# First half of a pooling stage and norm moved beside the last gathers, and four FFN blocks in plain fp32

## What is computed

```python
def block_fn(args):                                   # PEER
    tb, ib, gb = args
    u = u_tab[ib]
    act = jax.nn.gelu(jnp.einsum("td,thkd->thk", tb, u), approximate=False)
    vv = v_tab[ib]
    return jnp.einsum("thk,thkd->td", gb * act, vv)
x = _rmsnorm(x, normf_g)
for i in range(2):
    h = _modulate(_rmsnorm_2(x, norm_w[i, 0]), sh1, sc1)
    y = _pool_mixer(h, pool_w, pool_b, pool_scale)    # i == 0: window mean minus token, 256x256 per group
    x = x + g1 * y
    u = _modulate(_rmsnorm_2(x, norm_w[i, 1]), sh2, sc2) @ w_up
    up = u[t-1] * conv_w[0] + u[t] * conv_w[1] + u[t+1] * conv_w[2] + conv_b
    a, v = jnp.split(up, 2, axis=-1)
    x = x + g2 * ((silu(a) * v) @ w_down)
```

## Time and profile before

| what | us |
|---|---|
| median of 3 runs | 1671.11 |
| lowest, highest | 1670.04, 1671.52 |
| the profiled execution | 1669.39 |
| its span, first to last instruction | 1667.6 |

### The profile page before, as it was taken

How to read it: one execution, slowest core, us unless ns; L and a number is a source line. 1 busy time by engine, 2 the same in 40 slices (tenths; PEclk the granted TensorE clock), 3 DMA queues, 4 the chain that set the end, 5 groups by cost and what they waited for, 6 DMA issues and landing times.

```text
span 1667.6 us, 22193 instructions
## 1 busy us (share of the span) xinstructions
PE 1478.8 (89%) x8310; PEld 1059.6 (64%) x8310; DVE 1106.1 (66%) x2162; ACT 583.5 (35%) x847; POOL 824.9 (49%) x746
## 2 busy tenths in 40 slices
PE   8999999766565699999888885889999999999999
PEld 7997675654221266665443441438999896799987
DVE  4865633798488877877756675417886557468864
ACT  6653331211121222221100001127665454466652
POOL 0025230376767765656667777742675113036640
PEclk9999999987977899999799997999999999999999
DMA  7447860598999999999999999994555545635551
GB/s 281 152 151 301 318 253 26 210 389 304 393 407 371 409 401 402 402 403 403 401 401 394 409 396 402 406 396 161 171 187 190 189 182 222 243 111 202 176 191 38
DMA packets 154252, 477.15 MB, mean 286 GB/s; under 512 B 10017, under 2 KB 12321, under 8 KB 150945
## 3 DMA queue, kind: packets, MB, share of 16 engines
q0 software_dynamic: 73728, 268.47, 41.2%
q1 hardware_dynamic: 80416, 207.27, 34.0%
HBM read 474.65 MB, written 1.05 MB: 285 GB/s over the span
## 4 chain that ended last, share of the span: by engine, by line
PE 54%; DMA 13%; DVE 11%; POOL 10%; issue 5%; ACT 2%; DVEq 0%; ACTq 0%; POOLq 0%
PE ps L673 53%; DMA arena<-in_peer_v,cl 11%; POOL arena L2802 8%; DVE arena L1851 2%; PE ps L677 1%; POOL wring L2802 1%; DVE arena L1466 1%; DMA wring<-in_peer_v,cl 1%; DVE arena L1472 1%; DVE wring L1851 1%; DMA wring<-in_peer_u,arena 1%; DVE arena L1469 0%; DVE cvb L1472 0%; DVE arena L1781 0%; ACT arena L2190 0%
## 5 line engine op out<-in xcount | busy, mean ns | idle before, releaser
L673 PE MATMUL ps<-arena,wring 128*128 128x256 f32 (+2 forms) x2360 | 596.0, 488 | 106.0 <-DMA arena<-in_peer_v,cl 101.2
L673 PEld LDWEIGHTS ps<-arena,wring 128*128 128x128 f32 (+1 forms) x2360 | 333.0, 168 | 352.7 <-DMA arena<-in_peer_v,cl 179.7
L1851 DVE CUSTOM_DVE_ANT_0 arena<-arena 128x1024 f32<-128x1024 f32 x214 | 257.6, 1226 | 134.8 <-DMA arena<-in_peer_u,arena 131.9
L2802 POOL DMA_INDIRECT arena<-in_peer_u,arena x214 | 240.0, 1121 | 192.4 <-DVE arena L1809 78.2
L2802 POOL DMA_INDIRECT arena<-in_peer_v,cl x214 | 229.2, 1071 | 77.3 <-issue 60.4
L673 PE MATMUL ps<-hhl,wh 128*128 128x256 f32 (+1 forms) x1056 | 252.4, 323 | 1.2 <-POOL hhl L2812 0.7
L2190 ACT ACT_TABLE_LOAD x64 | 82.1, 1283 | 392.9 <-DVE arena L1851 266.1
L1466 DVE TENSOR_TENSOR wl<-wring,wh 128x2048 fp32r<-128x2048 f32 (+1 forms) x76 | 168.1, 2212 | 60.0 <-ACT wh L2193 58.2
L673 PE MATMUL ps<-hhl,wl 128*128 128x256 f32 x704 | 198.7, 282 | 0.0
L673 PEld LDWEIGHTS ps<-hhl,wh 128*128 128x128 f32 x1056 | 175.8, 190 | 19.5 <-POOL hhl L2812 2.5
L2193 ACT ACTIVATE wh<-wring 128x2048 fp32r<-128x2048 f32 (+1 forms) x78 | 146.1, 1874 | 70.7 <-PE ps L673 68.9
(11 more groups left out here) (257 smaller groups left out, 2025.4 us busy)
## 6 DMA issues: line engine op xcount, KB each, us to landing
wring<-in_ups SPq DMA_DIRECT2D x33, 2048.0 KB, 9.2
wring<-in_ada SPq DMA_DIRECT2D x24, 2048.0 KB, 9.9
wring<-in_ffn_w_down SPq DMA_DIRECT2D x12, 2048.0 KB, 9.0
wring<-in_w_in SPq DMA_DIRECT2D x8, 2048.0 KB, 8.3
wring<-in_ffn_w_down SPq DMA_DIRECT2D x6, 1536.0 KB, 7.6
wring<-in_peer_wq SPq DMA_DIRECT2D x4, 2048.0 KB, 16.1
wring<-in_attn_w_qkv SPq DMA_DIRECT2D x4, 2048.0 KB, 8.4
wring<-in_w_out SPq DMA_DIRECT2D x2, 2048.0 KB, 9.7
```

Of the source, the lines that this page charges most:

```text
L673: return pe.matmul(o, l, r, start=start, stop=stop)
L1851: ve.tensor_tensor_reduce(out=o, in0=o, in1=h2[:, t, :], scale=1.0, scalar=0.0, op0=MUL, op1=ADD, accum_out=dots[j % 2][:, k:k + 1]).then_ ...
L2802: po.indirect_dma_start(out=ring[n % NR], out_offset=None, in_=table, in_offset=bass.IndirectOffsetOnAxis(ap=which, axis=0)).then_inc(S[f" ...
```

## The change

Tokens 0 to 119 get their pooling stage and second norm ahead of the end of the gathers. A third list, `first`, is given to `woven` on PE, DVE and ACT, with 14 places between rest 458 and rest 517: the sums over the bands and the final norm's factors, then transposes, window products, pool products (120 columns), the norm's column sums, and on DVE and ACT the scaling and shift of these columns. Its rows lie in other memory (`y_a`, `z_a`). The pool weights are loaded into slot 1 ahead of the wait for `p_v` 248.

Behind the gathers PE begins with the first 120 columns of FFN blocks 0 and 1 in plain fp32 (`first_tokens`); then come window, transpose and pool products for tokens 120 to 255 (136 columns), the first 120 columns of block 2 on both sides of the norm sums (where four filler products stood), those of block 3, and then the other 136 columns of the four blocks (`direct_part`). Blocks 4 to 21 stay split; their pieces are counted from 0 again, so all later counts fall by four. The four direct blocks need no piece and no adding of a low sum; the pieces of blocks 4, 5 and 6 are prepared behind the norm and in `after` of blocks 0 to 2. The diff, cut:

```diff
-    nfb, junk = hpC[:, 1568:2592], hpC[:, 2592:3616]
+    nfb, y_a = hpC[:, 1568:2592], hpC[:, 2592:3616]
+    z_a = junk = hpC[:, 3616:4640]
+    NA, NB = 120, 136
...
-            if n == 496:
-                yield ("window_sums",)
-            elif n in (500, 504, 508):
-                yield "rows", (n - 500) // 4
+            if n == 500:
+                yield ("cleared",)
...
+    def woven(peer, context, first):
...
+        places = [458, 462, 466, 490, 492, 495, 497, 500, 502, 505, 508, 511, 514, 517]
...
+                if places and n == places[0]:
+                    places.pop(0)
+                    next(first, None)
...
-        nth[0] = 0
+        nth[0] = 1
+        load("pool", ("p_pl", 4), pool_w(), n=3)
         sp.wait_ge(*at("p_v", 248))
-        load("pool", ("p_pl", 4), pool_w(), n=3)
...
-                load(("up", l, g), split_done(n0 + 2 * g + 1), up(l, g), n=3)
+                direct = l == 0 and 2 * g < DIRECT
+                load(("up", l, g), ("p_dir", 2 * g + 2) if direct else split_done(n0 + 2 * g + 1), up(l, g), n=3)
...
-            busy(spread[:, 256:384], 4)
+            if between:
+                between()
+            else:
+                busy(spread[:, 256:384], 4)
...
+        def first_half():
+
+            pe.wait_ge(*at("d_l", 48))
+            for n in range(2):
+                b = take(("zb", n), "a_sz", 1)
+                for e in range(2):
+                    mm(b[:, 256 * e:256 * e + 256], ones, bands[2 * n + e][0], e == 0, False)
+                    k = mm(b[:, 256 * e + 120:256 * e + 256], ones, bands[2 * n + e][1], False, e == 1)
+            k.then_inc(S["p_zb"], 1)
+            for _ in range(3):
+                yield
+            pe.wait_ge(*at(*rows_at(0, "scaled")))
+            for q in range(2):
+                b = take(("xT", 0, q), "a_mb", q + 1)
+                for j in range(4):
+                    k = tr(b[:, c128(j)], y_a[:, c128(4 * q + j)])
+                k.then_inc(S["p_xT"], 1)
+
+            def windows_a(js):
+                for j in js:
+                    b = take(("wda", j), "v_pl", j + 1)
+                    for e in range(2):
+                        k = mm(b[:, 256 * e:256 * e + NB], z_a[:, c128(2 * j + e)], bands[j][0][:, 0:NB], True, True)
+                    k.then_inc(S["p_wda"], 1)
+
+            windows_a((0, 1))
+            yield
+            windows_a((2, 3))
+            yield
+            for half in range(2):
+                pooled(half, range(2 * half, 2 * half + 2))
+                yield
+            for _ in range(2):
+                yield
+            b = take("crsa", "a_crsa", 1)
+            pe.wait_ge(*at("a_csq", 4))
+            for c in range(8):
+                k = mm(b[:, 0:NA], ones, sqb[:, c, 0:NA], c == 0, c == 7)
+            k.then_inc(S["p_crsa"], 1)
+            yield
+
+        def pooled(t, gs, name="pla", n0=0, cols=slice(0, 120)):
+
+            w = weights("pool")[:, 0:2048].rearrange("p (g c) -> p g c", g=8)
+            n = cols.stop - cols.start
+            for g in gs:
+                pe.wait_ge(*at("v_pl", n0 + g + 1))
+                b = take((name, g), "v_px", 2 * n0 + 2 * g + 2)
+                for j in range(2):
+                    for kk in range(2):
+                        k = mm(b[:, 256 * j:256 * j + n], w[:, 2 * g + kk, c128(j)], sqb[:, 2 * g + kk, cols], kk == 0, kk == 1)
+                k.then_inc(S["p_" + name], 1)
+
         ring8[0] = [0, 1, 2, 3, 4, 7]
-        woven(peer(), context())
+        woven(peer(), context(), first_half())
...
+        direct = {}
+
+        def direct_part(f, i, cols):
+
+            w = weights(("up", 0, f // 2)).rearrange("p (k i c) -> p k i c", k=8, i=2)
+            for kk in range(8):
+                if f == i == 0 and cols.start:
+                    pe.wait_ge(*at("a_mid", mids(1, kk)))
+                k = mm(direct[f][:, 256 * i + cols.start:256 * i + cols.stop], w[:, kk, i, c128(f % 2)], sqb[:, kk, cols],
+                       kk == 0, kk == 7)
+            return k
+
+        def first_tokens(f, i):
+
+            if i == 0:
+                direct[f] = take(("up", 0, f), "v_up", f + 1, keep=True)
+                where["up", 0, f] = direct[f][:, 0:256], direct[f][:, 256:512]
+            direct_part(f, i, slice(0, NA))
+
+        pe.wait_ge(*at("a_cid", 32))
+        for f in range(2):
+            for i in range(2):
+                first_tokens(f, i)
+        wd = [take(("wd", j), "v_pl", 4 + j + 1) for j in range(4)]
         pe.wait_ge(*at("v_add", 2))
+        pe.wait_ge(*at(*rows_at(1, "pool")))
+        for j in range(4):
+            for e in range(2):
+                k = mm(wd[j][:, 256 * e:256 * e + NB], zrows[:, 1, c128(2 * j + e)], bands[j][1], e == 0, e == 1)
+            k.then_inc(S["p_wd"], 1)
+        pe.wait_ge(*at(*rows_at(1, "scaled")))
         for q in range(2):
             held[5 + q] = "a_mb", 3 + q
-        turned_rows(1, ps[5:7])
-        ring8[0] = list(range(7))
-        w = weights("pool")[:, 0:2048].rearrange("p (g c) -> p g c", g=8)
-        for g in range(4):
-            pe.wait_ge(*at("v_pl", g + 1))
-            b = take(("pl", g), "v_px", 2 * g + 2)
-            for j in range(2):
-                for kk in range(2):
-                    k = mm(b[:, 256 * j:256 * j + 256], w[:, 2 * g + kk, c128(j)], sqb[:, 2 * g + kk, :], kk == 0, kk == 1)
-            k.then_inc(S["p_pl"], 1)
+            where["xT", 1, q] = ps[5 + q]
+            for j in range(4):
+                k = tr(ps[5 + q][:, c128(j)], yrows[:, 1, c128(4 * q + j)])
+            k.then_inc(S["p_xT"], 1)
+        ring8[0] = list(range(8))
+        pooled(1, range(4), "pl", 4, slice(NA, 256))
...
+            start = 0
+            if l == 0:
+                start = DIRECT
+                first_tokens(2, 0)
+                token_norms(m, lambda: first_tokens(2, 1))
+                for i in range(2):
+                    first_tokens(3, i)
+                for f in range(DIRECT):
+                    for i in range(2):
+                        k = direct_part(f, i, slice(NA, 256))
+                    k.then_inc(S["p_dir"], 1)
+                    del kept["up", 0, f]
+                ring8[0] = list(range(7))
+            else:
+                token_norms(m)
+            for n in range(start, 22):
...
+                if l > 0 or blk >= DIRECT:
+                    ve.wait_ge(*at("a_lw", low_sums(l, blk)))
+                    k = tt(b[0][:, 0:256], b[0][:, 0:256], cv[:, 0, :], ADD)
+                    told(k, "v_us", low_sums(l, blk))
+                if l == 0 and blk in (1, 2):
+                    prepare(blk + 4)
+                elif blk > (4 if l == 0 else 0):
                     prepare(blk + 2)
...
+                scaled(m, lambda c: sqb[:, c, NA:256])
+                low = row_lo(rows_of[m], ffx[l], sqb)
+                for c in range(0, 8, 2):
+                    low(c)
+                prepare(DIRECT)
+            else:
+                scaled(m, lambda c: sqb[:, c, :], row_lo(rows_of[m], ffx[l], sqb, lambda c: mod(l, 3, c, 0)))
+                prepare(2)
...
+                direct = l == 0 and blk < DIRECT
+                ac.wait_ge(*at(*(("p_dir", blk + 1) if direct else ("p_u", n0 + blk + 1))))
                 if blk > 1:
                     ac.wait_ge(*at("g_act", 22 * l + blk - 1))
-                k = copy(cv[:, 0, :], where["up", l, blk][0][:, 256:512])
-                told(k, "a_lw", 22 * l + blk + 1)
+                if not direct:
+                    k = copy(cv[:, 0, :], where["up", l, blk][0][:, 256:512])
+                    told(k, "a_lw", low_sums(l, blk))
                 if blk > 0:
                     gate(blk - 1)
-                ac.wait_ge(*at("v_us", 22 * l + blk + 1))
+                if not direct:
+                    ac.wait_ge(*at("v_us", low_sums(l, blk)))
                 told(conv_mid(l, where["up", l, blk], cv, blk), "a_cv", 22 * l + blk + 1)
-                prepare(blk + 3)
+                if l == 0 and blk < 2:
+                    prepare(blk + 5)
+                elif not direct:
+                    prepare(blk + 3)
```

More of the change, by code:

```diff
@@ L101, in program @@
     ctx = ExitStack()
+    DIRECT = 4
     GOES_ON = {
@@ L1964, in context, with windowed, added_pool, first_half @@
             yield from modulated_c(2, lambda c: hcT[:, c, :], 1, 0)
-        woven(peer(), context())
+        def windowed(t, gs):
+            for g in gs:
+                ve.wait_ge(*at(("p_wda", "p_wd")[t], g + 1))
+                for e in range(2):
+                    c = 2 * g + e
+                    part = sqb[:, c, NA * t:NA * t + NB]
+                    k = stt(part, where[("wda", "wd")[t], g][:, 256 * e:256 * e + NB], AD[:, 0, 0, 0, c:c + 1], part, MUL, ADD)
+                told(k, "v_pl", 4 * t + g + 1)
+        def added_pool(t, gs):
+            o = slice(NA * t, (NA, 256)[t])
+            for g in gs:
+                ve.wait_ge(*at(("p_pla", "p_pl")[t], g + 1))
```

(72 more changed lines are left out.)

215 lines of the change are left out of this document (83 added, 132 removed).

## The result

The changed kernel takes 1679.29 us (median of 5 runs, 1677.09 to 1681.05) against 1671.05 beside it: a ratio of 1.0048, with a 95% interval of 1.0033 to 1.0063, that is 8.0 us slower (5.5 to 10.5). The forecast was 8.0 us slower, 1679.

The account below looks back on a forecast made before the run. Bound: in the last 60 us PE's order decides when gathers may be issued; later, PE itself. 2.8 + 5.6 - 0.4 = 8.0 us slower: 1677.4 against 1669.39, 1679 on the median's scale; range 1672.5 to 1684.

Parts of the forecast that it names:

- Part 1: Among the late gathers: the 1 MB pool weights, loaded earlier into a full DMA queue, cost 2.8 us (1.5 to 2.9).
- Part 2: Ahead of row 480: PE's inserted transposes, window and pool products delay gather issues, cost 5.6 us (3.0 to 6.6).
- the 0.7 us taken off for backlog at the end: At the last gathers: DMA backlog left there reduces the 6.3 us delay of gather 492's issue by 0.7.
- T: The moment PE's last products behind the gathers end, 1119.46 us before; forecast 8.4 us later, at about 1128.
- Part 3: From T to the steady FFN blocks: gain of about 0.4 us (ends: gain 3, loss 3.5).
- The wait ahead of block 7: In the FFN blocks: block 7 misses its low part by about 1.8 us, ACT waiting for POOL's late products.
- The first: Rival: the ring of twelve buffers hides the stops, POOL waits under 1 us at gather 492; 4.3 us faster; chance 0.08.
- The second: Rival: only the first POOL stop reaches the data (2.9), load paid, refund 2.5; 3.2 us slower; chance 0.14.
- a refund of 2.5: Time won back behind T, as the second rival put it; the first rival put it at 7.1 us.
- The third: Rival: up weights come at T + 4.7 and PE, having waited, runs slower; about 12.5 us slower; chance 0.15.
- Its price of 1.5 us for the lower clock: In the third rival: PE at its lower clock level after waiting loses some 1.5 us, read behind a 4.50 us wait.

Follow-up runs that it names:

- E1: The kernel before with only the pool weights' load moved ahead, right behind the context's last load; 1672.84 us, 1.0022.
- E6: Changed kernel with block 6's split behind block 2's convolution, windows at rest 482, transposes and pool products from rest 505; 1670.02 us, 1.0003.
- E13: E6 without the pool weights' load, its pool products reading what an earlier load left in the slot; 1665.9 us, 0.9983.
- E2: The kernel before with only PE's transposes, window and pool products inserted at the change's places, on constants, read by nobody; 1676.81 us, 1.0042.
- E8: The changed kernel run again unchanged, as reference on another chip; 1679.24 us, 1.0061 to the kernel before.
- E12: The kernel before with eight more products of 136 columns at rest 482, in PE's wait for gather 464; 1671.02 us, 1.0013.
- E10: E6 with the second load of up weights waiting until all 256 v rows are used instead of 248; 0.9999.
- E7: E6 with the pool weights issued later, when 218 v rows are used; 1670.68 us, 1.0006.

## Why the prediction was right

**Part 1, the megabyte: 2.8 forecast, 3.7 measured (E1, 2.0 to 5.2), 3.2 to 4.3 by the traces.** The mechanism is the one given: bytes among gathers that fill the DMA. The size was short, and so was the bound of 2.9: PE starts on gather 464 3.2 us later in E1 than before, and 3.1 later in E6 than in E13, which differ by the load alone. The 0.6 us of clock behind it and the last 0.5 us are not shown to be the megabyte's (E1). One reading was off: the load does not stand in front of gathers 464 to 467. In the changed kernel it is issued at 997.81 and lands 35.4 us later, before 464 is issued at 1047.62; it holds 464 back through the gathers ahead of that.

**Part 2, PE's inserted work: 5.6 forecast, 5.7 at the last sums (E2), 7.0 by the times (4.7 to 9.2).** The mechanism is the one given. That the two sizes agree to 0.1 is partly luck, since about 0.5 us of the 5.7 was lost ahead of the products. The issue of 486 was to come 3.0 us later and comes 3.3 later, 492 6.3 and comes 7.0. The shape of the stops was off: I put one of 6 us ahead of 486 and missed that the work at place 490 also stands ahead of rows 472 and 473, which gather 484 waits for. So it is 2.9 and 4.3 us, then 4.0 instead of 3. Their sum at the issue was nearly right, and the 0.7 us taken off for backlog at the end were 1.3 (7.0 at the issue, 5.7 at the last sums).

**T.** Forecast 8.4 later, at about 1128; it is 1129.30, 9.8 later on the trace's own scale and 10.6 counted from gather 400. By E1 and E2 the miss is mostly part 1's.

**Part 3, behind the last sums: gain of 0.4 forecast; a loss of 0.4 in the profiled execution, a gain of 1.1 in E8's.** Step by step: the up weights are there 1.15 us behind T (2.4); pool products end at 1146.0, T + 16.7 (16.6); block 4 starts at T + 44.1 (44.0). Block 5 waits 2.63 us (1.9), by the way that was named: the load for block 6, issued when block 1 has been used (T + 35.8; forecast 35.6), takes 10.29 us, then 1.93 on ACT, 2.30 on DVE and the taps. I had taken 8.9 from the earlier trace rows, the median of eight loads of the kernel before and not this load. By the rule of the Trainium skill that I set against it (DMA: Bandwidth & Descriptors, section on the anatomy of one DMA; an estimate of 6.8 us) block 5 would not have waited: the measurement decides, and it is further off than the row. The wait ahead of block 7 did not come (1.8 forecast): PE has none behind block 5. In its place the clock fell behind block 5's wait in the profiled execution, which cost 1.5 us against E8. Two errors of nearly one size cancelled there.

**The rivals.** The first needed a stop under 1 us ahead of 492; it is 3.98. The second needed PE's products to cost 2.9 us and a refund of 2.5; they cost 5 to 6 (E2), and the refund lay between -0.4 and 1.1. The third needed PE to wait 4.7 us for the up weights; it waited 1.15, and the clock stayed at 1.00 behind it. Its price of 1.5 us for the lower clock did not hold even where it was read, ahead of the key product (E12). E6 shows what was right in the first: with the steps in other places the stop ahead of 492 is gone, and what is left is the megabyte against the 4 us behind T, as that rival had said, only that the megabyte is nearly as large as the gain.

That the total is 8.0 forecast and 8.0 measured is luck. E1 and E2 add up to 10.7 us by the times and 10.0 at the last sums, the two profiled executions differ by 10.3 (1679.66 against 1669.39), and the same program run again (E8) is 10.1 us slower (7.8 to 12.4). All of this lies in the range, and the direction and the two causes are shown; the size is known to about 2 us.

## What to carry to other kernels

Work that is moved ahead to use an engine's idle time must be put where that engine waits, counted on its own list: PE waited about 4 us ahead of gather 464 and hardly at all in the forty us behind it; the products cost 5 to 6 us there (E2) and 0.7 in the pause and behind the late stretch (E13's last sums, one trace). Where a ring of buffers ties an engine's order to the issue of transfers, look for every transfer whose buffer stands behind the inserted step, not only for the first that stopped before. And bytes have a price of their own: a load that is moved from a slack stretch into one where the DMA is full is paid whole, whatever hides the rest.

## What the runs showed of the hardware

The clock behind a wait of PE is not a fixed price. Ahead of block 5 PE waited 2.63 us in the changed kernel's trace and 2.55 in E8's, the same program in another run; over the next 3.6 us the granted clock was 0.55 in the one and 1.00 in the other. The two rows (columns as above; PEclk is the third from the end):

```profile
1181.90:1185.50 3.60, 3.57 (x12) 3.04 (x13) 1.69 (x4) 1.93 (x4) 1.86 (x3) 0.55 1.02 393
```

E8:

```profile
1181.80:1185.40 3.60, 3.56 (x22) 3.21 (x23) 1.68 (x4) 1.93 (x4) 1.87 (x3) 1.00 1.04 397
```

The same with the windows in the pause ahead of gather 464, where PE had done the same work in each: behind 2.4 us of waiting the clock stayed at 1.00 in E6 and E10; it fell in E7 behind 2.23 us, and in E13, with E6's order on PE, behind 2.46 (0.51 over the next 3 us). E7, two us behind the wait:

```profile
1058.50:1061.00 2.50, 2.50 (x9) 0.71 (x7) 0.78 (x3) 0.00 (x0) 1.89 (x3) 0.50 1.03 408
```

What the lower clock costs depends on what follows: nothing ahead of the key product where it lasted under 3 us and the landings set the pace (5.68 us before, 5.69 in E6), 0.6 to 0.8 where it lasted about 5 (E1, E2), 1.5 us behind block 5, and 1.7 us in E12's pool products (8.83 instead of 7.15). A forecast should carry both.

A load of 2 MB among hardly any other traffic took 10.29 us in the changed kernel; eight such loads had a median of 8.9 before, and the nine issued between 1120 and 1240 us in the changed kernel one of 9.2.
